# Three pieces of the feed-forward gate's modulation moved from the scan levels to the norm behind the out-projection

## The reference

```python
def layer(x, ctx, mod_x, mod_c, ...):
    sh1, sc1, gt1, sh2, sc2, gt2 = jnp.split(mod_x[:, None, :], 6, axis=-1)
    ...
    hx = rmsnorm(x, g1) * (1 + sc1) + sh1
    ...                                    # in-projection, attention, gated linear attention
    x = x + gt1 * (jnp.concatenate([conv_x, attn_x, gla_x], axis=-1) @ w_out)
    x = x + gt2 * swiglu(rmsnorm(x, g2) * (1 + sc2) + sh2, w_up, w_down)
    ...

for l in range(2):
    mod_x = jax.nn.silu(c) @ w_mod[l] + b_mod[l]
    mod_c = jax.nn.silu(c_ctx) @ w_mod[l] + b_mod[l]
    x, ctx = layer(x, ctx, mod_x, mod_c, ...)
```

## Time and profile before

| | us |
|---|---|
| median of 3 runs (lowest, highest) | 2467.92 (2467.5, 2469.47) |
| the profiled execution, its time | 2468.22 |
| the profiled execution, its span | 2466.4 |
| PE busy of the span | 2402.3 |
| DVE busy | 1802.0 |
| ACT busy | 1479.1 |
| mean granted TensorE clock | 0.993 |

### The profile page before, as it was taken

The page is one execution under the profiler, slowest core; times in us unless marked ns, Lnnn a source line. Parts: engine busy times, 40 slices in busy tenths (PEclk is TensorE's granted clock), DMA queues, the critical chain, the costliest instruction groups (busy, mean ns, idle before and its releaser), DMA issues.

```text
span 2466.4 us, 38577 instructions
## 1 busy us (share of the span) xinstructions
PE 2402.3 (97%) x15096; PEld 2049.4 (83%) x15096; DVE 1802.0 (73%) x2443; ACT 1479.1 (60%) x1942; POOL 27.0 (1%) x86
## 2 busy tenths in 40 slices
PE   8999999999999899999999999999999999999998
PEld 5876788888887688898888889898888888888886
DVE  4556666566566677676666657579898898898997
ACT  4245365465444566556665545677777777777775
POOL 0000000000000000010000001000000000000000
PEclk9999999999999999999999999999999999999999
DMA  8247245555544545544245545147998998999996
GB/s 325 105 147 274 106 156 187 188 187 188 188 160 150 222 184 188 188 173 166 86 148 194 188 171 198 69 154 274 373 359 337 371 359 339 368 361 352 358 360 255
DMA packets 81641, 564.58 MB, mean 229 GB/s; under 512 B 9329, under 2 KB 12673, under 8 KB 13633
## 3 DMA queue, kind: packets, MB, share of 16 engines
q1 hardware_dynamic: 80144, 559.97, 60.7%
q0 software_dynamic: 1328, 2.25, 0.3%
HBM read 559.97 MB, written 1.05 MB: 227 GB/s over the span
## 4 chain that ended last, share of the span: by engine, by line
PE 88%; DVE 5%; ACT 4%; issue 1%; DMA 1%; SPq 0%; DVEq 0%; ACTq 0%
PE psum L247 86%; DVE ring_lo L241 2%; ACT ring_hi L238 2%; PE psum L740 1%; PE psum L2533 1%; DMA Z<-in_first_mods 1%; ACT hT L793 1%; DVE hT L839 1%; DMA ring<-in_stream 0%; DVE hT L1543 0%; ACT turned_probs L803 0%; DVE Z L1475 0%; ACT Z L803 0%; DVE Z L1472 0%; PE psum L1579 0%
## 5 line engine op out<-in xcount | busy, mean ns | idle before, releaser
L241 DVE TENSOR_TENSOR ring_lo<-ring,ring_hi 128x2048 fp32r<-128x2048 f32 x477 | 1092.1, 2290 | 272.8 <-ACT ring_hi L238 267.0
L238 ACT ACTIVATE ring_hi<-ring 128x2048 fp32r<-128x2048 f32 x477 | 912.3, 1914 | 333.4 <-PE psum L247 327.7
L247 PE MATMUL psum<-h_parts,ring_hi 128*128 128x512 f32 (+1 forms) x3184 | 861.4, 350 | 8.4 <-DVE h_parts L454 4.1
L247 PE MATMUL psum<-h_parts,ring_lo 128*128 128x256 f32 (+1 forms) x2464 | 601.7, 291 | 0.0
L247 PEld LDWEIGHTS psum<-h_parts,ring_hi 128*128 128x128 f32 x3184 | 516.1, 190 | 35.0 <-issue 11.3
L247 PE MATMUL psum<-ring_hi,h_parts 128*128 128x512 f32 (+1 forms) x1920 | 534.6, 365 | 0.4 <-ACT tok L324 0.4
L247 PEld LDWEIGHTS psum<-h_parts,ring_lo 128*128 128x128 f32 x2464 | 466.4, 189 | 72.4
L247 PEld LDWEIGHTS psum<-ring_hi,h_parts 128*128 128x128 f32 x1920 | 338.7, 189 | 52.5 <-ACT tok L324 0.8
L247 PE MATMUL psum<-ring_lo,h_parts 128*128 128x512 f32 (+1 forms) x960 | 347.4, 362 | 0.0
L247 PE MATMUL psum<-ring_hi,Zr 128*128 128x512 f32 (+1 forms) x736 | 225.3, 388 | 0.0
L247 PEld LDWEIGHTS psum<-ring_lo,h_parts 128*128 128x128 f32 x960 | 181.2, 189 | 28.8
(11 more groups left out here) (305 smaller groups left out, 2078.5 us busy)
## 6 DMA issues: line engine op xcount, KB each, us to landing
ring<-in_stream SPq DMA_DIRECT2D x524, 1024.0 KB, 4.8
Z<-in_first_mods SPq DMA_DIRECT2D x5, 1024.0 KB, 16.7
cst<-in_constants SPq DMA_DIRECT2D x1, 1216.0 KB, 8.1
mixT<-mixT POOLq DMA_DIRECT2D x32, 35.5 KB, 4.2
xT<-in_xT SPq DMA_DIRECT2D x1, 1024.0 KB, 6.2
xT<-in_ctxT SPq DMA_DIRECT2D x1, 1024.0 KB, 8.5
xT<-in_memT POOLq DMA_DIRECT2D x1, 1024.0 KB, 8.2
out_y<-hT SPq DMA_DIRECT2D x4, 256.0 KB, 2.5
```

What stands on the lines that cost most here:

```text
L238: e.activation(hi, raw, ACT.Copy).then_inc(sem("piece_rounded"), 1)
L241: e.tensor_tensor(lo, raw, hi.bitcast(F32), ALU.subtract).then_inc(sem("piece_split"), 1)
L247: ins = pe.matmul(*args, **kw)
```

## The change

Mod pieces 45 to 47 leave the levels. In the stream they come behind the four pieces of the out-projection and ahead of the feed-forward's first piece. The levels keep six pieces: 1, 2, 1 and 2 after levels 0 to 3. PE multiplies piece 45 after the out-projection and ahead of the mean, pieces 46 and 47 between the mean and the feed-forward, into bank 6. ACT copies the rows out after step 2 of the feed-forward, PE turns them after step 3, DVE takes the columns at step 4. The number of pieces and of matmuls with `c_mat` stays; one `act_rows_sum`, one `pe_columns_of` and one `dve_mod_take` are added.

```diff
-WINDOWS = (MOD_PIECES, 2 * MOD_PIECES - EARLY - MOD_PIECES)
+LATE_MODS = 3
+WINDOWS = (MOD_PIECES, 2 * MOD_PIECES - EARLY - MOD_PIECES - LATE_MODS)
...
-            + ["split"] * (4 + FFN_PIECES + 1 + CONV_AT) + ["conv"]
+            + ["split"] * 4 + ["mod"] * LATE_MODS + ["split"] * (FFN_PIECES + 1 + CONV_AT) + ["conv"]
...
         def gathered(layer, b):
-            return (IN_HEADS, IN_LEVELS)[b][layer]
+            return (IN_HEADS, IN_LEVELS, IN_NORM)[b][layer]
 
         def rows_sum(b):
-            return bank[6 + b][:, 0:256]
+            return bank[(6, 7, 6)[b]][:, 0:256]
 
         def columns_of(b):
-            return bank[7][:, 256 + 64 * b:320 + 64 * b]
+            return bank[(7, 7, 6)[b]][:, 256 + 64 * b:320 + 64 * b]
...
-        IN_LEVELS = (range(IN_HEADS[0].stop, MOD_PIECES + EARLY), range(IN_HEADS[1].stop, 2 * MOD_PIECES))
+        IN_LEVELS = (range(IN_HEADS[0].stop, MOD_PIECES + EARLY), range(IN_HEADS[1].stop, 2 * MOD_PIECES - LATE_MODS))
+        IN_NORM = (None, range(IN_LEVELS[1].stop, 2 * MOD_PIECES))
...
+        LATE_COLUMNS = 3
+
+        def pe_late_columns(pe, f):
+            if f == LATE_COLUMNS:
+                pe_columns_of(pe, 1, 2)
+
+        def dve_late_columns(dve, f):
+            if f == LATE_COLUMNS + 1:
+                await_next(dve, "mod_columns")
+                dve_mod_take(dve, 2, IN_NORM[1].start, IN_NORM[1].start, IN_NORM[1].stop)
+
         def act_mem_root(act, f):
+            if f == LATE_COLUMNS - 1:
+                act_rows_sum(act, 1, 2)
...
+                    pe_mod_add(pe, 1, 2, IN_NORM[1][0])
                     pe_mean(pe, 5, (5, 6, 7), 0, n)
-                    pe_ffn(pe, 2, between=lambda f: pe_mem_mean(pe, f))
+                    for m in IN_NORM[1][1:]:
+                        pe_mod_add(pe, 1, 2, m)
+                    pe_ffn(pe, 2, between=lambda f: (pe_late_columns(pe, f), pe_mem_mean(pe, f)))
...
-                    dve_ffn(dve, 2, 0, lambda q: gate_gain(1, 1)(q, 0), gained=True, between=lambda f: dve_mem_norm(dve, f),
+                    dve_ffn(dve, 2, 0, lambda q: gate_gain(1, 1)(q, 0), gained=True, between=lambda f: (dve_late_columns(dve, f), dve_mem_norm(dve, f)),
...
-            pieces += [by_columns(w), mods[EARLY + MOD_PIECES:], by_columns(out)]
+            pieces += [by_columns(w), mods[EARLY + MOD_PIECES:-LATE_MODS], by_columns(out), mods[-LATE_MODS:]]
```

## The result

The changed kernel took 2472.53 us (median of 13 runs, 2469.32 to 2473.91), the kernel before beside it 2467.6 (13 runs, 2463.26 to 2469.54): 4.9 us more by the medians. The ratio is 1.0025 with a 95% interval of 1.0018 to 1.0032, so the loss is clear of the noise, though small: it is as large as the 4.94 us that the prediction took as the least that one measurement can tell. The profiled execution took 2469.32 us, the lowest of the thirteen times, with a span of 2467.5. Its levels also started 2.7 us earlier than those of before (817.85 against 820.53), in code that the change does not touch. Half of it (1.35 us) arises where PE ran at the lower clock, some 23 us after the start, for 3.4 us instead of 6.8; most of the rest (1.06 us) near another such stretch at 250 us.

What follows compares the result with a forecast made beforehand. The chain of waits was taken as bound: PE in the feed-forward, PE, DVE and ACT alternating in the levels. -1.63 + 4.0 + 0.63 = +3.0 us on 2468.22, or 2470.9 against the median; range 2466.8 to 2474.0.

Steps and rivals of the forecast that it cites:

- The sum: Whole kernel: levels, transfers and feed-forward terms together, +3.0 us, bounds +0.4 to +4.4; chance as it stands 58%.
- the clock's case: Rival at the norm: PE's clock falls, feed-forward starts at half speed, 2.0 to 3.9 us on top of the forecast; 18%.
- The levels, less by 1.63: Levels: level 4 no longer waits for piece 47's transfer and product, 1.63 us gained, bounds 1.23 to 1.68.
- level 4 gains nothing: Rival in the levels: level 4's keys come as late as its products did, total +4.6 us, 2472.5; 6%.
- The transfers, 4.0 more: Out-projection's end: feed-forward's first two pieces land late and delay DVE's last add, 4.0 us more, bounds 2.1 to 5.0.
- f0 and f1 are hidden: Rival at the out-projection's end: feed-forward's first two pieces cause no delay, total -1.0 us, 2466.9; 8%.
- Pieces 45 to 47 at the norm, nothing: Norm: the three late products fit into PE's idle time around the mean and cost nothing.
- The feed-forward, 0.63 more: Feed-forward: PE's two small matmuls of four records stand where PE sets the pace, 0.63 us more, bounds 0 to 0.63.
- the low clock there gets shorter through the change: Rival behind the levels: low clock at 839 to 846 goes, at most 3.2 us back, total -0.2, 2467.7; 10%.

Runs made afterwards that it cites:

- e1: Changed kernel with mod pieces 45 to 47 neither loaded nor multiplied, only their bias kept; median 0.4 us under the kernel before, ratio 0.9996.
- e4: Changed kernel with four late pieces (44 to 47), one multiplied ahead of the mean, three behind; median 8.5 us over the kernel before, ratio 1.0046.
- e2: Changed kernel with only piece 47 late, multiplied behind the mean; median 2.0 us under the kernel before, ratio 0.9990.
- e3: Changed kernel with two late pieces (46 and 47), one multiplied ahead of the mean, one behind; median 0.7 us over the kernel before, ratio 1.0004.
- e7: Changed kernel with the splits of f0 and f1 one piece later in ACT's and DVE's lists; median 2.1 us under the kernel before, ratio 0.9998.
- e5: The changed kernel run once more, unaltered, for a second profile; median 4.5 us over the kernel before, ratio 1.0019.
- e6: Changed kernel with eight unused matmuls on constants between piece 45 and the mean; median 3.3 us over the kernel before, ratio 1.0020.

## Why the prediction came out as it did

The direction and the place were right: slower, by f0 and f1, with the levels' gain far too small to pay for them. The sum was +3.0 us; measured were +4.9 and, in the repeat, +4.5 by the medians. That is above the bounds of the sum itself (+0.4 to +4.4); it lies in the stated range because that took in a part of the clock's case, which came true in part.

- *The levels, less by 1.63.* Right: 1.64 in the changed kernel, 1.61 to 1.65 in every kernel with one to three late pieces, 1.63 with three left out (e1), 2.14 with four late (e4). The rival that level 4 gains nothing is out.
- *The transfers, 4.0 more.* The mechanism is shown by e2, e3, e4 and e7. The size was too small by 1.4: it is 5.4, and over its bound of 5.0. The step that failed is the landing of f0, taken as 6.6 us after its issue from a transfer at that place in the trace of before; it was 7.9 here and 7.9 to 8.0 in e5, e6 and e7, and some 1.4 us of that is one last part of the transfer (below). f1 landed after 4.9 as taken, but its rest on DVE then stood behind f0's. The rival "f0 and f1 are hidden" is what e2 is, with one piece.
- *Pieces 45 to 47 at the norm, nothing.* They did lie in the idle time: with the clock at 1.00 the way from mean to feed-forward is as long as before (e6). In the changed kernel itself the clock was low for the first 0.6 us of pieces 46 and 47. They took 2.20 us instead of 1.93 and still fitted: PE then waited 0.46 us for the first normed tile.
- *The feed-forward, 0.63 more.* 0.44: the chain's unbroken stretch on PE is 163.54 us with 935 records instead of 163.10 with 931. The chain of waits of the changed kernel has it as

```profile
899.70 163.54 PE psum L248 x935
```

- *The clock.* It fell where PE idled, as the rival said, but over the mean and the start of the late pieces and not over the feed-forward's start, so it cost 1.36 us and not 2.0 to 3.9. The sum had it at nothing. The Trainium skill, "TensorE: Matmul & The Clock Gate", section "HAM oscillation — how this bites in real kernels", has PE fall to the lower clock while it waits for a transfer and start its next work there. The two profiles of the changed kernel agree, with the mean at 0.50. The norm of before, where PE idled 0.81 us ahead of the mean, and e6, with 1.58 us, kept 1.00, so neither of these waits did it.

Put together from the profiles: -1.64 + 5.38 + 1.36 + 0.44 = +5.5 us. Against it stands that PE's low clock behind the levels lasted 835.8 to 839.3 in this profile (839 to 846 before), which made the way from level 4 to the out-projection 1.0 us shorter (14.13 instead of 15.14); in the repeat it was 14.65. That the low clock there gets shorter through the change, as one rival had it, stays open: it lasted 3.4 us in some of the experiments' profiles and 6.8 in others with the same code up to there, and the changed kernel itself had 3.4 in its first profile and 6.8 in e5. So some of the difference between the forecast and the measured number is chance.

## What to carry to other kernels

With a ring of slots, a piece inserted into the stream pushes the issue of every later piece to a later release; look up whose release that is, add the transfer's time, and compare with the moment at which the first engine asks for it. What a late piece costs is decided by what stands behind its wait in the lists of the in-order engines: the same late transfers cost 5.4 us as the lists stood and 1.5 with the splits one piece later, where f0's still stood ahead of the last piece's adds. The smallest step that removes the wait, here one piece of three, had nearly the whole gain of the levels (1.61 of 1.64 us) and made no engine wait for f0 or f1.

## What the runs showed that I had not expected

A 1 MB transfer lands in 16 parts, and its signal waits for the last. Of f0 in the changed kernel fifteen parts had landed by 865.86 us and the sixteenth at 867.29. While it was under way the queue for instructions moved one packet of 16 KB, at 864.48 for 0.95 us; the transfers' view of 864.4 to 864.6 has it:

```profile
q8 instruction: 1, 0.02, 29.8%
```

In the trace of before no such packet fell between 864.6 and 871.3. Between 800 and 900 us of the changed kernel's profile such packets stand 8 to 21 us apart. In e5, e6 and e7 f0's last part was late by 1.3 to 1.4 us in the same way; in e3, where the packet came at 867.23, f0 was whole within 0.4 us and f1's last part came 1.4 us behind the others. Piece 47 in the trace of before, the wait that the change removes, had fourteen parts there at 832.32 and the last at 833.73, with a packet at 830.20. Over the trace of the changed kernel from 60 us on the two go together, but not always: of 111 transfers with such a packet in the 4 us before their fifteenth part landed, 23 had their last part more than 0.9 us behind it; of 375 without a packet, 12 had. That the packet is what holds up the part is argued from this; no run moved it on purpose.
